# Two float32 transformer blocks on one core: three waits of GpSimd for VectorE in the seven-product turns, and one gated half moved

## What is computed

```python
h = norm(x) ...                                  # 1024 wide
u = _causal_depthwise_conv(h @ w_up, conv_w, conv_b)   # 1024 -> 5632, three taps along the positions
a, val = jnp.split(u, 2, axis=-1)
y = (jax.nn.silu(a) * val) @ w_down              # 2816 -> 1024
```

## Time and profile before

| what | value |
|---|---|
| median of 3 runs (each) | 1991.24 us (1986.69, 1991.24, 1994.27) |
| the profiled execution: its own time | 1996.07 us |
| its span | 1994.3 us |
| its mean granted PE clock | 0.99 |
| PE busy | 1926.6 us, 97% |
| DVE, ACT, POOL busy | 1235.6, 974.5, 1025.4 us |
| transfers | 222.99 MB, mean 112 GB/s |

### The profile page before, as it was taken

One profiled execution on the slowest core, in us unless ns is written; L12 is line 12 of the kernel. 1 busy time (PEld: TensorE's weight loads), 2 busy tenths in 40 slices (PEclk: granted clock), 3 DMA queues, 4 the chain that ended last, 5 costly groups with the idle time before them and its releaser, 6 DMA issues. The chain is left out here.

```text
span 1994.3 us, 35614 instructions
## 1 busy us (share of the span) xinstructions
PE 1926.6 (97%) x13706; PEld 1775.6 (89%) x13706; DVE 1235.6 (62%) x1854; ACT 974.5 (49%) x1650; POOL 1025.4 (51%) x612
## 2 busy tenths in 40 slices
PE   8999999999989999999999999899999998999897
PEld 6887888889879998999877999899999898999897
DVE  7964540227896783065677287888731678989702
ACT  3334433333656663255677454566533544666432
POOL 2536424442557764515565435687642246777542
PEclk9999999999999999999999999899999999999999
DMA  8932002221357743303100214677322114675321
GB/s 340 339 136 95 17 7 95 95 95 54 106 123 188 189 135 106 127 22 118 64 1 1 85 49 104 157 179 171 105 99 92 43 64 108 160 188 152 120 90 53
DMA packets 129893, 222.99 MB, mean 112 GB/s; under 512 B 8144, under 2 KB 97488, under 8 KB 129744
## 3 DMA queue, kind: packets, MB, share of 16 engines
q1 hardware_dynamic: 102560, 193.55, 29.1%
q0 software_dynamic: 25344, 25.17, 8.3%
q10 hardware_dynamic: 1840, 2.19, 0.4%
HBM read 218.78 MB, written 2.10 MB: 111 GB/s over the span
## 5 line engine op out<-in xcount | busy, mean ns | idle before, releaser
L1988 POOL TENSOR_TENSOR w_lo<-w_raw,w_hi 128x1024 fp32r<-128x1024 f32 x167 | 424.5, 2546 | 521.3 <-ACT w_hi L2260 495.4
L2260 ACT ACTIVATE w_hi<-w_raw 128x1024 fp32r<-128x1024 f32 (+2 forms) x299 | 290.5, 981 | 477.0 <-PE PS L1022 390.2
L2131 POOL TENSOR_TENSOR w_lo<-w_raw,w_hi 128x1024 fp32r<-128x1024 f32 x96 | 255.2, 2750 | 81.3 <-ACT w_hi L2260 81.3
L1022 PE MATMUL PS<-mid_hi,w_lo 128*128 128x256 f32 (+2 forms) x968 | 230.1, 296 | 8.8 <-DVE work L3603 4.7
L1847 PE MATMUL PS<-D_hi,w_lo 128*128 128x256 f32 (+2 forms) x768 | 219.7, 286 | 15.0 <-DVE w_lo L3695 10.7
L1022 PE MATMUL PS<-mid_hi,w_hi 128*128 128x256 f32 (+2 forms) x968 | 228.2, 294 | 0.0
L1022 PE MATMUL PS<-mid_lo,w_hi 128*128 128x256 f32 (+2 forms) x968 | 227.7, 293 | 0.0
L1847 PE MATMUL PS<-D_lo,w_hi 128*128 128x256 f32 (+2 forms) x768 | 219.1, 285 | 0.0
L1847 PE MATMUL PS<-D_hi,w_hi 128*128 128x256 f32 (+2 forms) x768 | 218.9, 285 | 0.0
L1022 PE MATMUL PS<-H_hi,w_lo 128*128 128x512 f32 (+3 forms) x672 | 204.4, 339 | 1.3 <-POOL w_lo L1988 1.0
L1022 PE MATMUL PS<-H_lo,w_hi 128*128 128x512 f32 (+3 forms) x672 | 203.3, 337 | 0.0
(11 more groups left out here) (464 smaller groups left out, 4758.3 us busy)
## 6 DMA issues: line engine op xcount, KB each, us to landing
w_raw<-stream SPq DMA_DIRECT2D x289, 512.0 KB, 3.5
ada_w<-ada SPq DMA_DIRECT2D x48, 512.0 KB, 7.0
w_raw<-stream POOLq DMA_DIRECT2D x24, 512.0 KB, 9.1
w_s<-stream SPq DMA_DIRECT2D x12, 512.0 KB, 5.4
w_s<-stream POOLq DMA_DIRECT2D x12, 512.0 KB, 6.9
w_s_odd<-stream SPq DMA_DIRECT2D x12, 512.0 KB, 5.4
w_s_odd<-stream POOLq DMA_DIRECT2D x12, 512.0 KB, 6.4
X<-xT SPq DMA_DIRECT2D x8, 256.0 KB, 5.6
```

Source lines behind the costliest of these rows:

```text
L1022: last = pe.matmul(out[:, c0 + a:c0 + b], w, x[:, a:b], start=start and i == 0, stop=stop and i == 2)
L1988: gp.tensor_tensor(w_lo[:, o], w_raw[:, o], w_hi[:, o].bitcast(F32), ALU.subtract)\
L2131: gp.tensor_tensor(t.part(w_lo, q), t.src(f, p), t.part(w_hi, q).bitcast(F32), ALU.subtract)\
L2260: return act_.activation(out, in_, ACT.Copy, scale=scale)
```

## The change

POOL: the transfer of the first turn's `s1` sum is issued before the last ordinary block's lowering instead of behind it. The four operand lowerings of turn 0 come together (the fourth had come behind that of product 4), and behind the first of them POOL waits until DVE has lowered product 2. In every turn it waits for DVE's lowering of product 5 before it lowers product 6, and for DVE's `sum2` of the next turn before it lowers the next turn's product 1. It makes one half of the gated product per turn; DVE makes the other behind its lowering of product 5. In layers 1 and 2 the first four down blocks wait, two and two, for `lower_mid` 0, 1 and 2, 3.

DVE: all four R operations stand before group 1's taps (there were two before, two behind). `sum2` of turn 0, and its lowering of product 2, stand before group 2's taps. The `signs` operation moves up. `sum2` of the next turn goes behind the first join of product 4 as before, in turn 0 behind the second. In the last turn `lower_mid` 0 and 1 come before the first join, and layers 1 and 2 do the last turn's first taps tile by tile. ACT does its roundings of turn 0 before group 2's taps. PE's and SP's lists are the same.

```diff
@@ lower_turns (POOL)
-                lower_blocks(BLK0[t.up] + b, t.w0)
+                lower_blocks(BLK0[t.up] + b, t.w0 - 1)
                 add_sums(t, 0, 1)
+                lower_blocks(t.w0 - 1, t.w0)
                 add_sums(t, 0, 3)
                 fast_lower(t, 0, 0)
                 fast_lower(t, 0, 1)
-                for d in range(3):
+                lower_operand(t, 0)
+                t.wait_lo(gp, 0, 2)
+                for d in range(1, 4):
                     lower_operand(t, d)
                 for f in range(FAST):
                     if f + 1 < FAST:
                         add_sums(t, f + 1, 1)
                     fast_lower(t, f, 4)
-                    if f == 0:
-                        lower_operand(t, 3)
-                    else:
+                    if f:
                         if f == FAST - 1:
                             t.wait_lo(gp, f, 3)
                         gated(t, CLASSIC + f - 1, 0)
-                        gated(t, CLASSIC + f - 1, 1)
+                    t.wait_lo(gp, f, 5)
                     fast_lower(t, f, 6)
                     if f + 1 < FAST:
                         add_sums(t, f + 1, 3)
                         fast_lower(t, f + 1, 0)
+                        t.wait_s2(gp, f + 1, 0)
                         fast_lower(t, f + 1, 1)
+            def lower_down(t, b):
+                a = BLK0[t.down]
+                gp.wait_ge(midl_ok, t.mid0 + 2)
+                lower_blocks(a, a + 2)
+                gp.wait_ge(midl_ok, t.mid0 + 4)
+                lower_blocks(a + 2, b)
...
-            lower_blocks(BLK0["down_b"], BLK0["pool"])
+            lower_down(sevens[1], BLK0["pool"])
...
@@ ffn (ACT)
-                for p in range(3):
+                for p in range(2):
                     fast_upper(t, 0, p)
-                for m in range(4):
...
-                for j in range(2):
-                    gate_silu(t, 2, j)
+                for d in range(4):
+                    round_operand(t, d)
+                fast_upper(t, 0, 2)
+                take(2, psum)
@@ ffn (DVE)
-                whole(0)
-                whole(2)
+                for k in range(0, KD, 2):
+                    whole(k)
+                if t.l == 0:
+                    signs()
                 body(1, psum)
-                whole(4)
-                whole(6)
                 operands()
+                sum2(0)
+                fast_lower(0, 2)
+                if t.l:
+                    signs()
                 taps(2, 0, lambda m: lambda a, b: psum(m)[:, a:b])
                 taps(2, 1, lambda m: lambda a, b: psum(m)[:, a:b])
-                fast_lower(0, 2)
                 gated(2, 0)
                 gated(2, 1)
-                signs()
                 for f in range(FAST):
...
                     fast_lower(f, 5)
-                    join(f, 4, 0)
-                    if f + 1 < FAST:
-                        sum2(f + 1)
-                    else:
+                    if f:
+                        v.wait_ge(mid_ok, t.mid0 + 2 * (g - 1) + 1)
+                        gated(g - 1, 1)
+                    if f + 1 == FAST:
                         lower_mid(0)
                         lower_mid(1)
+                    join(f, 4, 0)
+                    if 0 < f and f + 1 < FAST:
+                        sum2(f + 1)
                     join(f, 4, 1)
+                    if f == 0:
+                        sum2(1)
                     join(f, 5, 0)
                     join(f, 5, 1)
-                    taps(g, 0, lambda m: t.u(f, m))
+                    if t.l and f + 1 == FAST:
+                        first_by_tile(f)
+                    else:
+                        taps(g, 0, lambda m: t.u(f, m))
```

More of the change, by code:

```diff
@@ L2228, in _ @@
             lower_turns(sevens[2], RING)
-            lower_blocks(BLK0["down_c"], NBLK)
+            lower_down(sevens[2], NBLK)
             def over_root(k):
@@ L3630, in taps_two, with first_by_tile @@
                             chain.done(ins) if tap == 0 else ins.then_inc(free[m], 1)
+                def first_by_tile(f):
+                    g = CLASSIC + f
+                    for m in (0, 1):
+                        wait_first_tap(g, m)
+                        chain.done(tap_of(g, m, 0, t.u(f, m), max(t.a, 1), t.T))
+                        chain.wait()
+                        tap_of(g, m, 1, t.u(f, m), max(t.a, 2), t.T).then_inc(free[m], 1)
                 def taps_by_tile(f):
@@ L3685, in operands @@
                     chain.done(v.tensor_tensor(d7, b22, b12, ALU.subtract))
-                    sum2(0)
                     chain.wait()
```

## The result

The changed kernel took **1955.48 us** in the median of four runs (1954.69 to 1957.02), the kernel before 1990.46 in four: a ratio of 0.9825, 95% interval 0.9805 to 0.9845, so 35 us faster. 1956.4 had been forecast, with a range of 1946 to 1981.

The account below looks back on a forecast made before the run. PE, busy 97% of the span, was taken as the bound, so only its idle and low-clock time could be won. Terms -1.8 - 12.0 - 8.0 - 3.7 - 10.9 = -36.4 took 1992.8 to 1956.4 us; range 1946 to 1981.

Parts of the forecast that it names:

- Layer 0, before the turns: Ahead of group 2 of `up_a`: two R operations moved before group 1's taps cost 3.5 us idle, 1.7 clock: +5.2.
- Turns 0 and 1: Layer 0's first two up turns: `signs` and product 2's lowering move, product 3 is late next: -7.0 us.
- Layer 1, turn 0: First up turn of layer 1: DVE's lowering of product 5 is done 2 us early instead of late: -12.0 us.
- Layer 2, turn 0: First up turn of layer 2: the same gain as in layer 1's, -8.0 of 8.8 us.
- Later turns: Layer 2, turns 1 to 5: with one gated half off POOL, PE's waits, one per turn, go: -3.7 us.
- Ends: Last turn to down product, layers 1 and 2: POOL waits for `lower_mid`, taps free banks tile by tile: -10.9 us.
- Rival D: Slower: the waits tie DVE and POOL into one chain per turn, 21 later turns grow by 2.4 us: 2010; chance 0.07.
- The start of the sum: The time the terms were added to: 1992.8 us, the middle of the four executions shown of the kernel before.

## Why the prediction was right

The **mechanism** held: the two engines exclude each other, and the openings matter. It was shown by taking the waits away (+58), by putting them into the kernel before (-8) and, without any wait, by moving one issue (-47).

**Layer 0, before the turns** (+5.2 forecast): the idle was 3.66, as worked out (3.5). The 1.7 of clock did not come in this execution. **Turns 0 and 1** (-7.0): product 3 was the late one, ready at 573.0 instead of 574.1, and again no clock was lost. These two terms were 3.1 us too careful together. The path was not quite the one named: the second gated half was held for the last operand lowering only and was through at 569.4 instead of 572.7, and what was held for POOL's lowering for product 4 was product 3's own lowering, 3.60:

```profile
569.35 3.60 DVE L3707 TENSOR_TENSOR w_lo<-w_s,w_hi 128x1024 fp32r<-128x1024 f32 x1
```

The forecast also added up a low clock ahead of turn 0 and a late product 3. In the ten profiles that keep the wait ahead of group 2 these two never came together. The nine other profiled executions above all show 3.4 or 6.8 us at the low clock around it, and in none of them does PE wait for product 3 in layer 0. The kernel without the down waits has the same lists in this layer; group 2, then turns 0 and 1:

```profile
536.00:562.49 26.49, 23.94 (x96) 19.28 (x97) 20.70 (x22) 11.53 (x13) 14.26 (x7) 0.94 0.43 92
562.49:602.22 39.73, 39.73 (x338) 39.67 (x336) 31.23 (x36) 24.97 (x38) 31.74 (x15) 1.00 0.76 184
```

There product 3's lowering got in ahead of POOL's for product 4 and was through at 569.02, and from group 1's end to turn 2 it is 67.3 us, against 68.7 in the changed kernel's profile.

**Layer 1, turn 0** (-12.0): product 5's lowering was in time, 2.5 us early. What I missed is that product 3 is late there too, by 0.80, and by 1.55 in layer 2, its lowering held for POOL's of product 4, 3.62 and 4.37 long. I had carried the replay through in layer 0 only. **Layer 2, turn 0** (-8.0): the size was right, but "the same" was a misreading. Before the change PE waited there for product 3's lowering, behind `signs`:

```profile
1680.47 5.56 DVE L3668 TENSOR_SCALAR vec<-vec 128x48 f32<-128x48 f32 x1
...
1687.21 0.58 PE L1847 MATMUL PS<-D_hi,w_lo 128*128 128x258 f32 x1 [4.67 <-DVE w_lo L3695]
```

This stall belonged with the argument for layer 0, `signs` and product 2's lowering moved. In the kernel before with the waits, where nothing is moved, it shrank from 4.67 to 2.45 and stayed.

**Later turns** (-3.7): PE's waits for POOL in layer 2 went, but turns 1 and 2 of layer 1 grew by 0.7 us, which I had not priced. The price of the moved half on DVE I had put at nothing; in the changed kernel it is nothing because the waits stand around it, and without them it is 43 us.

**Ends** (-10.9): -12.5, nothing left of either stall. The size was right and the cause half wrong: "Taps and joins, which read PSUM, aren't held" is true of those that read PSUM, but taps of these layers also read `c` in SBUF, and those are held.

**Rival D** was worth more than its 0.07 as a mechanism, though not as an outcome. Its chain (a half held behind POOL's lowering of product 6, `sum2` behind the next run, joins late in most later turns) is much of what the kernel without waits does, though PE waits there for DVE's joins and not for POOL's `w_lo`, and `sum2` is held for two lowerings instead of one. That its 2010 is near the 2013 measured there is chance. I had put the blame on the waits; they are what prevents it.

The three terms that were too careful (by 4.7 us) and the four that were too bold (by 3.2) mostly cancel. The start of the sum was 2.3 us too high as well (1992.8 against a median of 1990.46), and the medians differ by 35.0 where the two profiled executions differ by 39.05. So the forecast of 1956.4 is nearer to 1955.48 than its terms deserve, and part of that is luck.

## What to carry to other kernels

Where VectorE and GpSimd both work on SBUF, a wait that idles GpSimd can be worth more than the work it delays: give each VectorE operation on the critical path a pause of GpSimd before it, or keep transfer issues from standing directly ahead of a run of GpSimd operations. Cost such a set of waits as a set, because taking out one moves the others' collisions. When a replay finds something late in one layer, carry it through the others before leaving them at nothing.

## What the runs showed of the hardware

An issue on GpSimd's queue ahead of two of its operations let both pass a waiting VectorE operation (`sum2` up to 6.94 us against 1.22 alone); with the issue moved, it took 3.43 at most, also between two operations that followed each other at once (3.09). A tiny VectorE operation on 48 columns in SBUF is held like a large one (2.45 us, and 5.47 behind an issue, against 0.17). Taps on an SBUF tile were held, 2.56 us, where the next one, the same but for its source in PSUM, took 0.48. Behind one and the same PE stall of 3.7 us the granted clock fell in nine executions and stayed at 1.00 in the tenth.
